# Splits of x by quarters at layer ends, S5 output tables ahead of input weights, key chain one slice later, last GLU split behind the first branch splits

## The reference, cut to what matters

```python
for i in range(DEPTH):                       # DEPTH = 2
    h = rmsnorm(x, norm_w[i])
    proj = h @ w_in[i]                       # u, gate | z, xBC, dt | q, k, v, gate | 3 merge gates
    y_s5  = s5_mixer(u, ...) * silu(s5_gate) # diagonal complex SSM, GELU, GLU
    y_ssd = ssd_mixer(z, xbc, dt_raw, ...)   # conv, chunked scan, gated RMSNorm
    y_att = window_attention(q, k, v, ...)   # QK-norm, partial rotary, sinks
    branches = einsum(stack(y_s5, y_ssd, y_att), w_branch[i])
    merged = sum(sigmoid(merge_logits) * branches)
    x = x + merged @ w_out[i]
```

## Time and profile before

| | us |
|---|---|
| median of three runs | 1995.85 (1995.22 to 1999.67) |
| the profiled execution: its own time | 1993.25 |
| its span, first to last instruction | 1991.5 |
| TensorE busy | 1911.2 |
| VectorE, ScalarE, GpSimd busy | 1311.9, 946.8, 530.2 |
| granted TensorE clock over the span | 0.99 |
| DMA | 372.78 MB, mean 187 GB/s |

### The profile page before, as it was taken

The page is one execution under the profiler, slowest core; times in us unless marked ns, Lnnn a source line. Parts: engine busy times, 40 slices in busy tenths (PEclk is TensorE's granted clock), DMA queues, the critical chain, the costliest instruction groups (busy, mean ns, idle before and its releaser), DMA issues.

```text
span 1991.5 us, 38600 instructions
## 1 busy us (share of the span) xinstructions
PE 1911.2 (96%) x13680; PEld 1704.9 (86%) x13680; DVE 1311.9 (66%) x1729; ACT 946.8 (48%) x1160; POOL 530.2 (27%) x578
## 2 busy tenths in 40 slices
PE   4998999999999999999979799999999999999998
PEld 4898999877777798889978799997777778988898
DVE  6855666687776757665567556667776766576654
ACT  5233333566656645333343333336656665543333
POOL 4105444262442000002411254452442410000033
PEclk9998999999999999999989999999999999999999
DMA  6345555555454456665544545555554554566656
GB/s 256 141 154 201 182 181 183 178 182 177 168 177 158 158 180 233 243 233 200 202 155 145 196 165 182 183 187 175 175 170 164 174 171 169 177 244 236 233 194 206
DMA packets 79442, 372.78 MB, mean 187 GB/s; under 512 B 20560, under 2 KB 27216, under 8 KB 40528
## 3 DMA queue, kind: packets, MB, share of 16 engines
q1 hardware_dynamic: 76560, 359.99, 51.8%
q0 software_dynamic: 1088, 6.80, 0.8%
q10 hardware_dynamic: 1696, 4.72, 0.6%
HBM read 351.80 MB, written 21.76 MB: 188 GB/s over the span
## 4 chain that ended last, share of the span: by engine, by line
PE 83%; DVE 6%; issue 4%; DMA 2%; ACT 2%; POOL 1%; SPq 1%; DVEq 0%; ACTq 0%; POOLq 0%
PE mm L1602 13%; PE mm L1604 13%; PE mm L1603 13%; PE mm L1561 11%; PE mm L1562 11%; PE mm L1563 11%; DMA raw<-in_stream 2%; DVE w_lo L974 1%; ACT w_hi L687 1%; PE b L1698 1%; PE by L1762 1%; PE bs L1708 1%; PE b L1753 1%; PE bs L1714 1%; PE b L1774 1%
## 5 line engine op out<-in xcount | busy, mean ns | idle before, releaser
L687 ACT ACTIVATE w_hi<-raw 128x2048 fp32r<-128x2048 f32 x299 | 571.4, 1911 | 696.0 <-DMA raw<-in_stream 685.0
L974 DVE TENSOR_TENSOR w_lo<-raw,w_hi 128x2048 fp32r<-128x2048 f32 x299 | 690.4, 2309 | 245.7 <-ACT w_hi L687 236.8
L1561 PE MATMUL mm<-h_lo,w_hi 128*128 128x256 f32 x2240 | 644.5, 288 | 37.6 <-DVE h_lo L978 37.3
L1562 PE MATMUL mm<-h_hi,w_lo 128*128 128x256 f32 x2240 | 637.4, 285 | 0.0
L1563 PE MATMUL mm<-h_hi,w_hi 128*128 128x256 f32 x2240 | 637.2, 284 | 0.0
L1561 PEld LDWEIGHTS mm<-h_lo,w_hi 128*128 128x128 f32 x2240 | 433.9, 194 | 42.1 <-DVE h_lo L978 37.5
L1562 PEld LDWEIGHTS mm<-h_hi,w_lo 128*128 128x128 f32 x2240 | 433.8, 194 | 1.5 <-issue 1.0
L1563 PEld LDWEIGHTS mm<-h_hi,w_hi 128*128 128x128 f32 x2240 | 433.5, 194 | 0.0
L1602 PE MATMUL mm<-w_lo,h_hi 128*128 128x512 f32 x768 | 317.2, 413 | 0.0
L1604 PE MATMUL mm<-w_hi,h_lo 128*128 128x512 f32 x768 | 301.1, 392 | 0.0
L1603 PE MATMUL mm<-w_hi,h_hi 128*128 128x512 f32 x768 | 299.8, 390 | 0.0
(11 more groups left out here) (309 smaller groups left out, 2319.5 us busy)
## 6 DMA issues: line engine op xcount, KB each, us to landing
raw<-in_stream SPq DMA_DIRECT2D x300, 1024.0 KB, 4.8
gscr<-gt SPq DMA_DIRECT2D x48, 256.0 KB, 6.0
gin<-gscr SPq DMA_DIRECT2D x24, 512.0 KB, 5.6
bd<-in_bdense SPq DMA_DIRECT2D x16, 384.0 KB, 5.2
lam<-lscr SPq DMA_DIRECT2D x128, 32.0 KB, 2.7
x_old<-out POOLq DMA_DIRECT2D x2, 2048.0 KB, 9.7
out<-proj ACTq DMA_DIRECT2D x8, 512.0 KB, 6.3
proj<-in_x SPq DMA_DIRECT2D x4, 512.0 KB, 8.3
```

The lines of the kernel that those rows point to most:

```text
L687: e.activation(w_hi[:, j % RAW, :], raw[:, j % RAW, :], ACT.Copy).then_inc(hi_done, 1)
L974: e.tensor_tensor(w_lo[:, j % RAW, :], raw[:, j % RAW, :], w_hi[:, j % RAW, :].bitcast(F32), ALU.subtract).then_inc(lo_done, 1)
L1561: e.matmul(out, whi, xlo, start=start, stop=False)
L1562: e.matmul(out, wlo, xhi, start=False, stop=False)
```

## The change

- Start: ScalarE takes the squares and the split of a quarter of x together, and converts slot 0 after the first quarter, slots 1 and 2 after the last. VectorE weighs two quarters, takes the remainder of the first, makes w_lo of slot 0, then alternates, with w_lo 1 and 2 last. The constants are loaded behind slot 2 instead of slot 1.
- Layer end: the last four output pairs leave the loop. TensorE signals each quarter of h that the last pair has read (h_free); ScalarE splits quarters 0 to 2 of the new x meanwhile and quarter 3 after the last tile; VectorE takes remainders 0 and 1 before it copies the last pair's output, 2 and 3 after it, then w_lo of the slot that it had before them. The splits at the top of the layer go.
- Input part: tanh and silu of the B/C tiles a slice later, with two buffers bt; k_ss after pair 8, k_v and the inverse root at n = 9, kn at n = 10, k_rot after pair 12, k_fin at 13, gm at 14, the kscr DMA at 14.
- s5_tile, in all tiles: cl0 to cl2 ahead of bw0 to bw3; kv waits for both.
- glu_hi(3) and glu_lo(3) move behind the first conversion (ScalarE) and the first branch sums (VectorE); the wait for glu_lo3 on ScalarE goes.

No matmul, no load and no conversion is added or removed.

```diff
         sd = al("sd", [P, 8, 32])
         kk = al("kk", [P, 4, 2 * TOK])
...
+            for j in range(1, RAW):
                 e.dma_start(raw[:, j, :], stream[j]).then_inc(landed[j], 16)
+                if j == 2:
+                    e.dma_start(cst[:], consts).then_inc(const_in, 16)
...
                 at_c = PP["c_re"][0]
                 c2 = par[:, at_c:at_c + 2 * ST * 16].rearrange("p (r s) -> p r s", r=2)[:, :, bass.ds(i * 64, 64)]
+                W.wait(SP, "KV", 1)
                 W.wait(SGp, "frac")
+                W.settle()
                 SGp.mark(e.tensor_copy(cl[:, :, :, 0, :], c2.rearrange("p r (j h) -> p r j h", j=4)), "cl0")
...
                     SGp.mark(e.tensor_tensor(to, to, tc, ALU.subtract if r else ALU.add), f"cl{r + 1}")
                     W.wait(SGp, f"cl{r + 1}")
+
+                b2 = bd[:, 0:2 * TOK].rearrange("p (r c) -> p r c", r=2)
+                e.wait_ge(s5_w, e.snap((L * 8 + i + 1) * 144))
+                W.settle()
+                SGp.mark(e.tensor_tensor(bw[:], b2, both(lam[:, 0, :]), ALU.mult), "bw0")
+                W.wait(SGp, "bw0")
+                SGp.mark(e.tensor_tensor(b2, b2, both(lam[:, 1, :]), ALU.mult), "bw1")
...
+            squares(0)
+            split_x(0, 0)
+            hi(0, 0)
+            squares(1)
+            split_x(0, 1)
+            squares(2)
+            split_x(0, 2)
+            squares(3)
+            split_x(0, 3)
+            hi(0, 1)
+            hi(0, 2)
...
-                e.wait_ge(pair_done, e.snap(L * N_LAYER + SPLIT))
-                for q in range(4):
-                    e.wait_ge(x_w, e.snap(L * 16 + (4 * q + 4)))
-                    LA.mark(e.activation(h_hi[:, 4 * q:4 * q + 4, :], proj[:, 32 + 4 * q:36 + 4 * q, :], ACT.Copy), f"xhi{q}")
...
+                    if 5 <= n < 9:
+                        t = n - 5
-                        if t:
-                            W.wait(LV, f"bc_silu{t - 1}")
-                        LA.mark(e.activation(bt[:], kk[:, 2, 0:TOK] if t % 2 == 0 else kk[:, 2, TOK:], ACT.Tanh, scale=0.5), f"bc_tanh{t}")
+                        if t >= 2:
+                            W.wait(LV, f"bc_silu{t - 2}")
+                        LA.mark(e.activation(bt[:, t % 2, :], kk[:, 2, 0:TOK] if t % 2 == 0 else kk[:, 2, TOK:], ACT.Tanh, scale=0.5), f"bc_tanh{t}")
+                    if n == 9:
-                    if n == 13:
+                    if n == 14:
...
-                glu_hi(3)
-                W.wait(LV, "glu_lo3")
...
                     hi(nb, 2 * n + LEAD)
+                    if n == 0:
+                        glu_hi(3)
                     hi(nb, 2 * n + 1 + LEAD)
...
-                with e.Fori(0, 4) as I:
+                with e.Fori(0, 3) as I:
...
+                made, passed_by, next_w = e.snap(L * 16), e.snap(L * 3), e.snap(L * 16 + 16)
+                for j in range(4):
+                    if j < 3:
+                        hi(nb, j + LEAD)
+                    else:
+                        for q in range(3):
+                            e.wait_ge(h_free, passed_by + (q + 1))
+                            e.wait_ge(x_w, next_w + (4 * q + 4))
+                            e.activation(h_hi[:, 4 * q:4 * q + 4, :], proj[:, 32 + 4 * q:36 + 4 * q, :], ACT.Copy).then_inc(x_hi, 1)
+                    e.wait_ge(x_new, made + (13 + j))
+                    W.settle()
+                    e.activation(proj[:, 28 + j, :], proj[:, 12 + j, :], ACT.Square).then_inc(x_sq, 1)
+                e.dma_start(xs_out[L + 1][:, 12:16, :], proj[:, 12:16, :]).then_inc(x_out, 16)
+                e.wait_ge(x_w, next_w + 16)
+                e.activation(h_hi[:, 12:16, :], proj[:, 44:48, :], ACT.Copy).then_inc(x_hi, 1)
+                hi(nb, 3 + LEAD)
...
+            def rest_x(base, q):
+
+                e.wait_ge(x_hi, base + (q + 1))
+                tt_(h_lo[:, 4 * q:4 * q + 4, :], proj[:, 32 + 4 * q:36 + 4 * q, :],
+                    h_hi[:, 4 * q:4 * q + 4, :].bitcast(F32), ALU.subtract).then_inc(x_lo, 1)
...
+            weigh(0)
+            weigh(1)
+            e.wait_ge(x_w, 4)
+            rest_x(0, 0)
+            lo(0, 0)
+            weigh(2)
+            e.wait_ge(x_w, 8)
+            rest_x(0, 1)
+            weigh(3)
+            e.wait_ge(x_w, 12)
+            rest_x(0, 2)
+            e.wait_ge(x_w, 16)
+            rest_x(0, 3)
+            lo(0, 1)
+            lo(0, 2)
...
+                    if 6 <= n < 10:
+                        t = n - 6
                         W.wait(LA, f"bc_tanh{t}")
-                        LV.mark(e.scalar_tensor_tensor(proj[:, BC + t, :], bt[:], 1.0, bc_dst(t), ALU.add, ALU.mult), f"bc_silu{t}")
+                        LV.mark(e.scalar_tensor_tensor(proj[:, BC + t, :], bt[:, t % 2, :], 1.0, bc_dst(t), ALU.add, ALU.mult), f"bc_silu{t}")
+                        if t >= 2:
+                            W.wait(LV, f"bc_silu{t - 2}")
-                    if n == 8:
+                    if n == 9:
-                    if n == 9:
+                    if n == 10:
-                    if n == 13:
+                    if n == 14:
-                    if n == 12:
+                    if n == 13:
...
-                glu_lo(3)
...
                     branch(n, 1)
+                    if n == 0:
+                        glu_lo(3)
...
-                with e.Fori(0, 4) as I:
+                with e.Fori(0, 3) as I:
...
+                made, split, next_w = e.snap(L * 16), e.snap(L * 4 + 4), e.snap(L * 16 + 16)
+                for j in range(4):
+                    if j == 3:
+                        e.wait_ge(x_w, next_w + 12)
+                        rest_x(split, 0)
+                        rest_x(split, 1)
+                    e.wait_ge(pair_done, nb + (j + 3))
+                    tt_(proj[:, 12 + j, :], mm[:, j % 2, 0:256], x_old[:, 12 + j, :], ALU.add).then_inc(x_new, 1)
+                    e.wait_ge(x_new, made + (13 + j))
+                    W.settle()
+                    e.tensor_scalar(proj[:, 44 + j, :], proj[:, 12 + j, :], flat(nw[:, bass.ds(L + 1, 1), 12 + j:13 + j]), None,
+                                    ALU.mult).then_inc(x_w, 1)
+                    if j < 3:
+                        lo(nb, j + LEAD)
+                e.wait_ge(x_w, next_w + 16)
+                rest_x(split, 2)
+                rest_x(split, 3)
+                lo(nb, 3 + LEAD)
...
+                    if after and k % 4 == 3 and k < KT - 1:
+                        ins.then_inc(after, 1)
...
-                    W.wait(LV, f"xlo{q}")
+                    e.wait_ge(x_lo, x_parts + (q + 1))
...
-                    if n == 7:
+                    if n == 8:
                         W.wait(LA, "k_sq")
                         LP.mark(e.matmul(b7[:], C("blk"), kk[:, 0, :], start=True, stop=True), "k_ss")
-                    if n == 11:
+                    if n == 12:
                         W.wait(LV, "kn")
...
+                        W.wait(SGp, "bw3")
                         W.wait(SGp, "cl2")
...
-                with e.Fori(0, 3) as I:
+                with e.Fori(0, 2) as I:
...
+                nb = e.snap(L * N_LAYER + (N_OUT + 12))
+                read = e.snap(L * 16 + 11)
+                for j in range(4):
+                    e.wait_ge(x_new, read + j)
+                    pair(nb, j, None, h_free if j == 3 else None)
```

More of the change, by code:

```diff
@@ L300, in program @@
         x_w = sem("x_w")
+        h_free = sem("h_free")
+        x_hi = sem("x_hi")
+        x_lo = sem("x_lo")
         x_sq = sem("x_sq")
@@ L363, in _ @@
                     e.dma_start(raw[:, 0, :], stream[0]).then_inc(landed[0], 16)
-            e.dma_start(raw[:, 1, :], stream[1]).then_inc(landed[1], 16)
-            e.dma_start(cst[:], consts).then_inc(const_in, 16)
-            for j in range(2, RAW):
+            for j in range(1, RAW):
                 e.dma_start(raw[:, j, :], stream[j]).then_inc(landed[j], 16)
+                if j == 2:
+                    e.dma_start(cst[:], consts).then_inc(const_in, 16)
             e.dma_start(xs_out[0], x).then_inc(x_copied, 16)
@@ L699, in inv_sqrt, with split_x, squares @@
                 S_.mark(e.activation(out, logs, ACT.Exp, scale=-0.5), name + "_r")
-            for m in range(KT):
-                if m % 4 == 0:
-                    e.wait_ge(x_in[m // 4], 16)
-                e.activation(proj[:, 16 + m, :], proj[:, m, :], ACT.Square).then_inc(x_sq, 1)
-                if m in (3, 7, 11):
-                    hi(0, m // 4)
+            def split_x(L, q):
+                e.wait_ge(x_w, L * 16 + (4 * q + 4))
+                e.activation(h_hi[:, 4 * q:4 * q + 4, :], proj[:, 32 + 4 * q:36 + 4 * q, :], ACT.Copy).then_inc(x_hi, 1)
+            def squares(q):
+                e.wait_ge(x_in[q], 16)
+                for m in range(4 * q, 4 * q + 4):
+                    e.activation(proj[:, 16 + m, :], proj[:, m, :], ACT.Square).then_inc(x_sq, 1)
+            squares(0)
[9 more added lines that the diff above has]
+            hi(0, 2)
```

(6 more changed lines are left out.)

39 lines of the change are left out of this document (12 added, 27 removed).

## The result

The changed kernel takes 1973.24 us (median of four runs, 1967.26 to 1975.94) against 1996.12 (1995.22 to 1999.67) of the kernel before, timed beside it: a ratio of 0.9873, 95% interval 0.9848 to 0.9898 (the quotient of the two medians is 0.9885). It is 23 us faster where 50 were forecast, and outside the range of 1934 to 1962. The profiled execution took 1972.46 us, its span is 1970.7, 20.8 shorter than that of before.

What follows compares the result with a forecast made beforehand. TensorE, busy 1911 of 1991.5 us, bounds the kernel; only its idle time can be won. Terms 7.9 + 4.7 + 15.5 + 16.5 + 5.3 = 49.9 us off the median 1995.85 give 1946.0 us, range 1934 to 1962.

Steps and rivals of the forecast that it cites:

- six idle places: Six places where TensorE stands idle, together 72.2 of the 80 us that it isn't busy; only this time can be won.
- the branch term: Last GLU split moved, so the wait before the second branch product goes: saving 5.3 us, 3 to 5.6.
- S5 tables, the later tiles: A layer's other seven tiles: the moved tables run right after the taps, beside VectorE's back and scan; no cost counted.
- D: Rival: the later tiles' output tables delay VectorE and stall TensorE, slower, up to 84 us in 14 tiles, 2030; chance 0.02.
- Key chain: Input pairs: waits at the key sums and key rotation go, less 2 us of new stalls: saving 15.5 us, 9 to 17.5.
- rival B: Conversions become the bound, VectorE stays behind in the input stages, with waits for its copies at pairs 10 to 13: 1956; chance 0.16.
- Start: Before the first layer's pairs: TensorE starts near 15.9 instead of 26.1, sum of squares ends at 26; saving 7.9 us, 5 to 9.
- Layer end: Between layers 0 and 1: gap of 11.2 us becomes 6.5, the cost of TensorE's jump; saving 4.7 us, 0 to 12.4.
- rival A: The jump at the layer boundary costs TensorE and the norm chain nothing, 7.7 us more saved: 1938; chance 0.12.
- First tiles: A layer's first S5 tile: tables made early, 2.2 us stall left behind the taps (1.7 in layer 1); saving 16.5 us, 13 to 18.

Runs made afterwards that it cites:

- e1: Changed kernel, but in the gate loop's four S5 tiles GpSimd makes the input weights ahead of the output tables again: 1956.24 us, ratio 0.9802.
- e4: Changed kernel, but the output tables of tiles 0 to 3 wait until VectorE has finished the key chain: 1965.14 us, ratio 0.9846.
- e9: Changed kernel with the input weights ahead of the output tables in all eight tiles, as before the change: 1964.20 us, ratio 0.9853.
- e7: Changed kernel with the key chain put back where it was, with one buffer bt: 1986.06 us, ratio 0.9957.
- e11: Changed kernel with the edits of e1, e4 and e8 together: 1944.45 us, ratio 0.9757.
- e6: Changed kernel, but at the start GpSimd adds only the first 8 of 16 squared tiles into ssum: 1965.84 us, ratio 0.9846.
- e10: Changed kernel with a back-edge hint on the layer loop for all five engines: 1972.73 us.
- e3: Changed kernel with bw0 and bw1 each made by two instructions of half the columns: 1963.85 us, ratio 0.9839.
- e8: Changed kernel, but SyncE issues the load of slot 18 ahead of the first S5 tile's 17 small DMAs: 1969.39 us, ratio 0.9870.

## Why the prediction was wrong

**The bound, right.** The six idle places were the right ones, and all were filled about where the working said: the first matmul at 14.97 (15.9), pair 0's end at 27.2 (25.2), no wait at the key sums, 1.89 us behind the taps (2.2), the branch term exact.

**S5 tables, the later tiles: the step that failed.** The prediction knew the mechanism and made a rival of it (D), but judged it by w_lo beside the short table products (2.34 instead of 2.28 us) and by the states' margin. The term for the later tiles was put at nothing. The working should have asked what else moves when the tables go ahead: the weights, two products of 1.3 us each, go *behind*, to where VectorE makes qn, w_lo and stt. It also priced D as all or nothing in 14 tiles, 84 us. It struck in six iterations (three a layer, slots 57, 69, 81) at about 2.3 us each, with one half clock on top: 15.7 us, of which e1 gave back 14.3. D's chance of 0.02 was that of a total of 2030, not of its mechanism.

**Key chain: the cover was mis-sized.** "Seven operations at up to 0.5 us of delay each" was right for one layer as a bound, but I took 2 us of stalls for both, where they cost 7 (e4), the far end of the stated 0 to 7. The wait before pair 10 is rival B's sign. B's reason, that VectorE is late by its own work, was a smaller part: the waits before pair 10 are 6.3 us in both layers, 2.2 with the tables away (e4), and 1.8 with their order undone (e9). The chain itself gave 13 of 15.5 (e7), and 15.7 without the collisions (e11).

**Start: wrong in ssum.** Pair 0 should by its own price (2.6 us a quarter from 15.9) have ended at 26.3, not 25.2; it ended at 27.2. The larger miss is the sum. I had additions of 0.9 us beside weighing, and of 1.8 for the last eight, starting at 14.9, and put the end at 26, at most 29. It was 31.67: all twelve took 1.69, likely since VectorE now has remainders and w_lo between the weighings from the first quarter on (no run takes these away alone). ss came 2.8 us earlier than before instead of some 8, and 2.3 of that went to the clock. e6 shows that the additions held it; that the rest of the chain had room was right.

**Layer end: wrong in the jump.** TensorE's was priced at 6.5 us by ScalarE's row. It took 1.9 (e10), and no half clock followed, which wasn't sure: in e3 the same 1.9 us were followed by half clock for 3.4 us. This is rival A's side, 5.3 us to the good.

**First tiles: 12.6 for 16.5.** The wait behind the taps was as forecast. What was missed is the collision of the next tile's weights with the states, with its own wait of 1.4 us, and 2.8 us behind the taps in layer 1 (forecast 1.7). Behind these 2.8 us half clock stood for 3.4 us, where the prediction had none behind waits of 2.8; it had read that from the waits of the kernel before. With e8's order in SyncE's queue and the collisions away the term comes out, 17.5 us (e11).

## What to carry over

When work is moved on an engine that shares the ports with another, list both what comes earlier and what is thereby pushed later, and lay each against the other engine's timeline; the price is the length of the instruction that is running when the critical one arrives. Put the long instructions of the engine with slack where the critical engine has long ones of its own or idles, or cut them in pieces. And reorder only the tile that needs it: here one tile in eight gained (12.6 us in both layers), and three others lost more than that (15.7).

## What was not expected of the hardware

An addition on 128x2 on VectorE took 1.25 us, and a one-input step on 32 columns 0.66 instead of 0.17, with a GpSimd product running: here the delay didn't follow the size of the delayed instruction. Idle stretches of 1.8 us were followed by half clock in the first gate iteration (0.71 in the stage from 410.4 to 416.3) and not in the five like it, so this cost came and went. So it was elsewhere. TensorE waited 2.6 us before pair 10 in the changed kernel, and 2.8 us at the rotation of the keys in the kernel before. The stage behind the first, columns as in the earlier trace rows:

```profile
96.80:102.00 5.20, 5.20 (x31) 5.20 (x32) 5.20 (x6) 2.92 (x2) 0.00 (x0) 0.67 0.32 135
```

Its mean granted clock was 0.67, that behind the second (115.1 to 120.0 us) 1.00. And one hint at a loop's top removed two engines' idle time of 4.3 and 1.9 us, with no gain that the times can show.
